# State space loop of a two-block model on one Trainium2 core: the two products with the imaginary table become one, on a sum that GpSimd makes

## What is computed

```python
def s5_mixer(u, lam_re, lam_im, log_dt, b_re, b_im, c_re, c_im, d, w_glu):
    ...
        bur = jnp.einsum('gnh,btgh->btgn', bb_r, uc)
        bui = jnp.einsum('gnh,btgh->btgn', bb_i, uc)
        ...
        pr, pi, sr, si = lax.associative_scan(combine, (ar, ai, bur, bui), axis=1)
        xr = sr + pr * cr[:, None] - pi * ci[:, None]
        xi = si + pr * ci[:, None] + pi * cr[:, None]
        y = jnp.einsum('ghn,btgn->btgh', c_re, xr) - jnp.einsum('ghn,btgn->btgh', c_im, xi)
    ...
    y = y + d.astype(f32) * u.astype(f32)
    y = jax.nn.gelu(y).astype(u.dtype)
    ab = y @ w_glu
```

## Time and profile before

| | |
|---|---|
| Time, median of 3 runs | 1722.12 us (1722.08 to 1727.5) |
| The profiled execution | 1726.02 us, its span 1724.1 us |
| Mean granted TensorE clock | 0.996 |
| PE busy | 98% of the span |
| DVE, ACT, POOL busy | 50%, 44%, 56% |
| The loop in the span | about 572 us to 655 us |

### The profile page before, as it was taken

The page is one execution under the profiler, slowest core; times in us unless marked ns, Lnnn a source line. Parts: engine busy times, 40 slices in busy tenths (PEclk is TensorE's granted clock), DMA queues, the critical chain, the costliest instruction groups (busy, mean ns, idle before and its releaser), DMA issues.

```text
span 1724.1 us, 20954 instructions
## 1 busy us (share of the span) xinstructions
PE 1698.1 (98%) x8056; PEld 1399.4 (81%) x8056; DVE 869.5 (50%) x1250; ACT 763.1 (44%) x1203; POOL 969.2 (56%) x606
## 2 busy tenths in 40 slices
PE   9999999999999999999999999999999999999998
PEld 7888888777778898888888888887678888888887
DVE  3999997757787785522212121485644221212124
ACT  5333335476867763343222223443664332323234
POOL 5858755657678575654444445664556444444464
PEclk9999999999999999999999999999999999999999
DMA  4322323222245234222222222222112222222221
GB/s 168 106 99 86 111 97 123 90 73 95 86 181 195 67 124 134 98 98 98 98 95 94 95 97 98 89 95 98 38 50 99 98 96 94 95 96 97 98 98 61
DMA packets 56258, 172.65 MB, mean 100 GB/s; under 512 B 6496, under 2 KB 14816, under 8 KB 55264
## 3 DMA queue, kind: packets, MB, share of 16 engines
q1 hardware_dynamic: 56160, 171.33, 28.7%
HBM read 165.01 MB, written 6.29 MB: 99 GB/s over the span
## 4 chain that ended last, share of the span: by engine, by line
PE 68%; DVE 6%; ACT 3%; issue 2%; POOL 2%; DMA 1%; SPq 0%; DVEq 0%; ACTq 0%; POOLq 0%
PE B L315 57%; PE B L2439 1%; PE B L2441 1%; PE B L2437 1%; PE B L2314 1%; PE B L2235 1%; PE B L2335 1%; PE B L298 1%; DVE SW L1150 1%; DVE B L1016 1%; PE B L300 1%; PE B L299 1%; PE B L2411 0%; PE B L2405 0%; PE B L2407 0%
## 5 line engine op out<-in xcount | busy, mean ns | idle before, releaser
L291 POOL TENSOR_TENSOR WL<-RAW,WH 128x1024 fp32r<-128x1024 f32 x281 | 681.5, 2427 | 610.0 <-ACT WH L287 609.7
L287 ACT ACTIVATE WH<-RAW 128x1024 fp32r<-128x1024 f32 x281 | 296.7, 1058 | 627.3 <-PE B L315 595.5
L315 PE MATMUL B<-P0h,WH 128*128 128x512 f32 x1096 | 428.6, 391 | 4.1 <-ACT WH L287 2.3
L315 PE MATMUL B<-P0l,WH 128*128 128x512 f32 x1096 | 422.2, 390 | 0.4 <-DVE P0l L432 0.3
L315 PE MATMUL B<-P0h,WL 128*128 128x512 f32 x1096 | 276.4, 389 | 0.0
L315 PEld LDWEIGHTS B<-P0h,WH 128*128 128x128 f32 x1096 | 206.0, 188 | 48.8 <-DVE Yl L428 2.6
L315 PEld LDWEIGHTS B<-P0l,WH 128*128 128x128 f32 x1096 | 206.0, 188 | 43.2 <-DVE P0l L432 1.1
L315 PEld LDWEIGHTS B<-P0h,WL 128*128 128x128 f32 x1096 | 205.7, 188 | 42.8
L439 DVE TENSOR_TENSOR H<-H,B 128x512 f32<-128x512 f32 x88 | 60.2, 686 | 288.2 <-PE B L315 288.1
L315 PE MATMUL B<-P1h,WH 128*128 128x512 f32 x448 | 174.7, 390 | 0.0
L1967 DVE SCALAR_TENSOR_TENSOR TMP<-B,RS 128x512 f32<-128x512 f32 x64 | 44.1, 691 | 258.4 <-PE B L315 244.1
(11 more groups left out here) (354 smaller groups left out, 2699.5 us busy)
## 6 DMA issues: line engine op xcount, KB each, us to landing
RAW<-in_w SPq DMA_DIRECT2D x281, 512.0 KB, 3.2
PX<-in_zeros SPq DMA_DIRECT2D x4, 1024.0 KB, 9.8
H<-in_xT SPq DMA_DIRECT2D x8, 256.0 KB, 5.3
U<-u SPq DMA_DIRECT2D x32, 64.0 KB, 2.0
g<-GB SPq DMA_DIRECT2D x8, 256.0 KB, 2.2
GB<-g SPq DMA_DIRECT2D x32, 64.0 KB, 2.0
out<-Q SPq DMA_DIRECT2D x4, 512.0 KB, 3.6
CA<-in_zeros SPq DMA_DIRECT2D x1, 1920.0 KB, 10.0
```

Source lines behind the costliest of these rows:

```text
L287: act.activation(WH[:, i % NS, :], RAW[:, i % NR, :], ACT.Copy).then_inc(*inc("w_hi", i))
L291: pool.tensor_tensor(WL[:, i % NS, :], RAW[:, i % NR, :], WH[:, i % NS, :].bitcast(F32), ALU.subtract).then_inc(*inc("w_lo", i))
L315: return pe.matmul(b[:, :], w[:, ws[c]], x[:, c, :], start=start, stop=stop)
```

## The change

For each chunk, POOL adds X3 to X2 in place (`pool_state`) as soon as the state is announced, and PE does three products of `CA` per tile instead of four. The products of `TT`, X0 and X1 of all four tiles come first, then a wait for the sum, then the four products of the imaginary table. As products of one tile are no longer neighbours, only the first product of the bank carries `start`.

```diff
@@ pe_y @@
         pe.wait_ge(*at("tt_copy", ("tt", q)))
         pe.wait_ge(*at("state", ("v", q, 1)))
+
+        def product(i, g, stop=False):
+            return pe.matmul(b[:, 128 * g + 1:128 * g + 128], CA[:, z, i // 2, g, 1:5, :].rearrange("p m h -> p (m h)"),
+                             X[:, q % 2, i, g, 0:127], start=False, stop=stop, skip_group_check=True)
         for g in range(4):
-            pe.matmul(b[:, 128 * g:128 * g + 128], TT[:, z, g, :], U4[:, q % 4, g, :], start=True, stop=False)
-            for i in range(4):
-                last = pe.matmul(b[:, 128 * g + 1:128 * g + 128], CA[:, z, i // 2, g, 1:5, :].rearrange("p m h -> p (m h)"),
-                                 X[:, q % 2, i, g, 0:127], start=False, stop=i == 3)
+            pe.matmul(b[:, 128 * g:128 * g + 128], TT[:, z, g, :], U4[:, q % 4, g, :], start=g == 0, stop=False,
+                      skip_group_check=True)
+            for i in range(2):
+                product(i, g)
+        pe.wait_ge(*at("state_sum", q))
+        for g in range(4):
+            last = product(2, g, stop=True)
         last.then_inc(*inc("y_mm", q))
+
+    def pool_state(pool, q):
+        x = [X[:, q % 2, i, :, :].rearrange("p g c -> p (g c)") for i in (2, 3)]
+        pool.wait_ge(*at("state", ("v", q, 1)))
+        pool.tensor_tensor(x[0], x[0], x[1], ALU.add).then_inc(*inc("state_sum", q))
@@ pool_ssm @@
             if q + 3 < 8:
                 pool_u(pool, q + 3)
+            pool_state(pool, q)
             if q > 1:
                 g_lo(pool, q - 2)
```

## The result

The changed kernel takes 1732.31 us (median of 6 runs, 1728.79 to 1735.47) against 1722.43 for the one before (6 runs); the ratio is 1.005, interval [1.004, 1.0061]. By the medians it is 9.9 us slower, by the means 8.7 us, where 6.6 were forecast. In a later session the same pair gave 1731.7 against 1723.8, ratio 1.0042 [1.003, 1.0054]: 7.9 us.

A forecast was written before the change was run, and what follows sets the result against it. The GpSimd-ScalarE ring was taken to set the loop's end, with PE's work counting only from there. Of 7.1 us saved 0.9 counts; +5.8 waiting and +1.7 clock give +6.6 us, 1728.7 us, range 1725.5 to 1732.5.

The forecast's parts named there:

- forecast 1.6, 2.2, 6.3: Chunks 3, 4 and 5: PE idle about 1.6, 2.2 and 6.3 us ahead of the imaginary products, for GpSimd's sums.
- The ring: GpSimd's g_lo and tables, then ScalarE's copies and next rounding of g: 10.5 us per chunk, slower than PE; predicted unmoved.
- +5.8 of the forecast: Chunk 5: the late sum makes pe_v(7) start at 638.6 instead of 632.85, 5.8 us later.
- the forecast had 4.9: End of pe_y(6), 646.1 instead of 641.24: 5.8 of waiting less 0.9 saved in that chunk, +4.9 us on the path.
- +6.6: Predicted change of the whole kernel's time: 6.6 us slower, with a chance of 0.47.
- one drop, 1.7: Behind chunk 5's long wait: one fall of the granted clock, costing 1.7 us on pe_v(7) to pe_y(6).
- rival B: Clock falls twice, or additions last 1.45 us, or ScalarE is met: +8.3 to +9.5, 1730.4 to 1731.6 us; chance 0.25.
- 0.9 us saved in chunk 7, counted at nothing: pe_y(7): its saved 0.9 us only lengthen PE's idle time before chunk 6 of glu, from 0.9 to 1.8 us.
- D: Rival: PE bounds the loop throughout and all 7.1 us saved come out, 1715.0 us; chance 0.04.
- C: Rival: chunk 5's addition is made in time, so not slower, 1721.2 us; chance 0.10.
- the place 632.85: Arrival of chunk 7's input and start of pe_v(7) before the change; a sum at 631.9 would leave it there.
- the gain of 0.9 us: pe_y(6): the only saving that would count if chunk 5's addition came in time, 0.9 us.

The follow-up runs named there:

- e11: The changed kernel measured again unaltered, in a later session: 1731.7 us, ratio 1.0042 to the kernel before.
- e8: The kernel before, all twenty products and no additions, but in the change's product order and with chunk 5 waiting for the first glu low part: 1731.64 us, 1.0041.
- e2: The changed kernel with only chunk 5's addition moved, behind chunk 4's and ahead of the glu low part in GpSimd's list: 1726.87 us, 1.0017.
- e1: The changed kernel without the additions and without PE's wait for them, so the output lacks X3: 1725.38 us, 1.0011.
- e3: The changed kernel with 25 idle products on PE ahead of chunk 5's wait, filling it: 1731.27 us, 1.0043.
- e4: The changed kernel with the additions made by VectorE instead of GpSimd: 1729.82 us, 1.0033.
- e5: The changed kernel with additions 3 to 6 re-placed in GpSimd's list, so none but the last stands behind a glu low part: 1727.23 us, 1.0015.
- e6: e5 with SP sending g(6) ahead of the fetch that waits for the third glu low part: 1724.67 us, 1.0002.

## Why the prediction was right, and where it was short

**The mechanism.** Right in each of its places. PE waits in chunks 3, 4 and 5 for 0.72, 2.01 and 6.11 us (forecast 1.6, 2.2, 6.3; in e11 1.44, 2.02, 4.49), and each time for L1701. In chunk 3 the wait is shorter than forecast because PE had already lost part of what it saved at waits for its input: 1.89 us ahead of `pe_v(3)` (0.24 before) and 0.66 ahead of `pe_v(4)`. The addition of chunk 5 stands behind the low part of the first glu unit. The ring did not move: `g_lo` is where it was, shifted by the 0.87 us. The addition of chunk 6 ended 643.53 + 1.27 = 644.8, which PE didn't wait for. e8 shows that this wait alone makes a loss of the same size, e2 that removing it brings most of it back.

**Where the time went,** from the table: v(7) +6.62, made of the +5.8 of the forecast and +0.9 for the eight rows of chunk 5 behind the wait, which ran at 1.2 GHz (636.73 to 638.60 is 1.87 us). From there to glu +0.67: `pe_v(7)` +1.6, its products in chunk 6 -0.9. To chunk 6 +0.26, in the two transfers of g(6). Sum +7.55: 2.5 for the clock and some 5.0 for the rest, where the forecast had 4.9. Then the low stretch from 662.77, +1.6. The profiled spans differ by 6.5 us only, since the loop began 0.87 us earlier (the trace before has a low stretch at 8.0 us that this one lacks) and the trace before has another at 1199.3, right behind the last row, that this one lacks too. That the spans agree with +6.6 is therefore luck; the medians differ by 9.9 and 7.9.

**The step that was short** is the term of the clock, "one drop, 1.7". In the profiled execution the drop at the long wait lasted 6.83 us and cost 2.5, and a second came behind the wait for g(6), with 1.6. Together 4.1 us, so that rival B, given 0.25, tells better what happened than the forecast, given 0.47. 4.9 + 4.1 makes 9.0 against the measured 9.9 and 7.9. The prediction had both parts in hand (the wait for g(6) growing to 1.8 us was in its text; 1.99 were measured), and treated the second as less likely. Seven traces have this wait at 1.78 to 2.01 us; behind four of them (after, e1, e3, e11) comes a low stretch, behind three (e2, e4, e5) none. The other seven have it at 1.08 us or less, and none has a low stretch behind it. So PE's 0.9 us saved in chunk 7, counted at nothing, lengthen a wait behind which 1.6 us were lost in four traces of seven. That the length of the wait is what does it is likely by these counts, and not shown by a run of its own.

**The base.** 1722.1 us was the median of three runs of a kernel that has four levels (below) and a median of 1723.6 over 84 later runs. Part of the 9.9 is that first session.

**Rivals.** D is refuted by e1. C, the addition made in time, was tried as e2 and e5. With v(7) at 51.86 and 52.91 against 51.10 they came to within 0.8 and 1.8 us of the place 632.85, but the gain of 0.9 us never came, since other waits took it: for the sum of chunk 6 in e2, for the input of chunk 7 in e5.

## What to carry to other kernels

An operation given to an engine that is half idle costs by its place in that engine's list: here 1.28 us of work, whose input VectorE had ready at 623.3, started at 635.41 and came 6 us late for PE, because it stood behind an operation that waited for a third engine. So before moving work, look in the receiver's timeline for what stands ahead of it at each iteration, the last ones above all, where other work is interleaved. And work taken off an engine that then waits for others only makes its waits longer. In e1 that ended in a lower mean clock and no gain at all.

## What was not expected of the hardware

- **The clock makes levels.** Over the five later sessions the kernel before reads 1721.94 us at a mean granted clock of 0.999 (median of 15 runs), 1723.54 at 0.998 (41), 1725.24 at 0.997 (16) and 1726.28 at 0.996 (12): about 1.5 us for each thousandth. A low stretch of 3.41 us at half speed is just 1.7 us, a thousandth of the span. The traces show the same price at one place: from the first product of chunk 6, 888 rows of products last 201.9 to 202.0 us in the four traces with a low stretch there and 200.2 to 200.4 in the other ten, 1.6 us less. The changed kernel's twelve runs lie between 0.996 and 0.992. With medians of 0.998 and 0.995, some three low stretches more at 1.5 us are 4.6 us, and with the 4.9 of waiting 9.5 us. The division isn't exact: a low stretch that falls into idle time lowers the mean clock and costs nothing, and at 0.996 the changed kernel's three runs (1728.71 to 1730.09) are only 2.4 to 3.8 us above the kernel before.
- **Contention of VectorE and GpSimd.** In e4 an addition of two SBUF operands, 128x512, takes 0.69 us on VectorE by itself, 1.10 to 1.17 beside GpSimd's operations on 128x320 and 128x512 and up to 2.67 beside its low part on 128x1024. GpSimd's 128x320 operation goes from 0.86 to 1.19 us.
- **A 16 KB instruction packet** within 1.5 us behind the issue of a 256 KB transfer goes with 2.8 to 4.3 us instead of 2.0 for it, and a sixteenth of the data, eight or nine packets, comes behind it (e5). Something like it happens at the very end. In e4, e6 and e11 such a packet starts 2.6 us behind the last product, among the transfers of the output, and the execution ends 8.8 us behind that product. In the other eleven traces none starts between the last product and the end, and it ends 7.05 us behind. These 1.7 us have nothing to do with the loop, and they stand in e11's profiled execution of 1734.9 us.
